# A hybrid decoder layer on one core: the branch merge passes through PSUM, and the last two experts reach their tokens by one-hot matmuls

## The chip, the core and the metric

One core of a Trainium2 chip: TensorE (PE, the matrix engine; PEld is its weight load), VectorE (DVE), ScalarE (ACT), GpSimd (POOL) and SyncE (SP, which here only issues DMAs), with SBUF and the eight banks of PSUM. The metric is the device time of one execution in microseconds. Before: 993.0 us, the median of 3 runs (991.35 to 993.85).

## The reference, cut to what matters

512 tokens of width 1024, one layer. Two things of it matter here: the merge of two attention branches, and the mixture of experts (each token goes to two of 32 experts, inside one of four groups, and their weighted outputs are added to the residual).

```python
h = rms_norm(x, g_norm_mix[l]) * (1 + scale1) + shift1
proj = h @ w_in[l]
...
g_dil, g_sb = jnp.split(jax.nn.sigmoid(h @ w_branch_gate[l]), 2, axis=-1)
merged = g_dil * (o_dil @ w_branch_dil[l]) + g_sb * (o_sb @ w_branch_sb[l])
x = x + gate1 * (merged @ w_out[l])
h2 = rms_norm(x, g_norm_ffn[l]) * (1 + scale2) + shift2
y = hierarchical_moe(h2, ...)   # silu(xe @ w_g[e]) * (xe @ w_u[e]) @ w_d[e], top-1 group, top-2 experts
x = x + gate2 * y
```

## The kernel before, in words

Each engine has its own instruction stream, written out by hand, and they meet only in semaphores. SP's queue issues nearly all loads in program order. The stages follow one another:

**Start and projections.** x is normalised and transposed; `w_ada` is multiplied by the conditioning vector in three rounds of eight pieces. Round one comes first; rounds two and three are woven into the 24 projection units (`for u in range(NU)` on TensorE): after each of the first 16 units comes one w_ada piece of 1 MB, through the single buffer `ada_slot`, whose next load SP issues when the piece has been used. Halves of `w_in` (1 MB, rows of 1 KB) are loaded between them. Weights and activations are split into a high and a low part, so each product is three fp32r passes (`split_product`, whose matmuls carry line L669). ACT makes the high part, DVE or GpSimd the low one (`split_lo`, L557 on GpSimd). `mod_round(1)` on DVE closes the second round, and copies the first gate into `grow`, which until then held the arguments of the rotary sines.

**Attention and merge.** TensorE computes the dilated and the stick-breaking attention and the gates. The merge goes over f, eight chunks of 128 channels by 512 tokens, each two products with `w_branch_sb` (`sb_product`, L853, PSUM bank f % 4). DVE multiplies by the gate (L1693), writes SBUF, and adds the other branch (L1696) into `hT`. ACT copies that to the high part (L1307), GpSimd subtracts for the low part (L581). ACT and GpSimd have the split of the second half of w_out (`split_hi(11, ..)`, `split_lo(11, ..)`) queued ahead of that. Then TensorE broadcasts the first gate over the partitions (L891), waits until ACT has copied it out (L1311), broadcasts the second (L898), computes the router bias (L906) and starts the eight output products, u = 0 to 7 (L669). DVE multiplies each by the gate (L1720) and adds x (L1724).

**Routing.** From the logits DVE makes rank tables: each expert has 64 slots (`CAP`); if an expert had more than 64 tokens, further rounds would run in `more_rounds`. Here none runs.

**Experts.** 32 experts, three weight buffers of 6 MB in `arena`. SP loads expert e + 3 as soon as TensorE has used the parts of expert e (waits on `gu_ps` and `dn_ps`); the first ones wait for `br_ps`, `o_ps` and `lg_ps`. Per expert TensorE gathers the 64 tokens' rows by a one-hot matrix (L1001), transposes them, and multiplies by gate and up (L1024); ACT and DVE compute the SwiGLU; TensorE transposes and multiplies by down (L1043). Both products use only 64 columns of the array, in pairs that run side by side. DVE weighs the result (L1886) into `ye`, GpSimd copies the expert's slot indices (L600) and stores the rows to `y_rows` in HBM by an indirect DMA (L603). `y_rows` has two rows of 512 for each of a token's two experts.

**End.** The order is in the straight-line code behind the loops: expert 31 has three idle matmuls (`keep_clock(3)`, L967) between its hT transposes (L1033) and its down product. When all 32 stores have landed, SP reloads `y_rows` in four tiles (L473), DVE adds the two y of each token to x (L1965, L1966), and SP stores the output. The sum x itself is rebuilt from its two parts by `whole_x1` (L1857).

Of the kernel before, what the change touches and what calls it, by code (L numbers as in the profile page):

```python
# [14 lines left out]
P = 128  # L15
D = 1024
# [44 lines left out]
def hybrid_layer(nc, x, c, positions, w_ada, b_ada, g_norm_mix, g_norm_ffn, w_in, w_branch_gate,  # L61
# [6 lines left out]
    with ctx:  # L68
# [161 lines left out]
        x1n = arena[:, EXP_W:EXP_W + NT * D].rearrange("p (t n) -> p t n", t=NT)  # L230
        wcol = sb("wcol", [P, 1])
# [31 lines left out]
        gn_T = sem("gn_T")  # L263
# [3 lines left out]
        mod_cols = sem("mod_cols")  # L267
# [20 lines left out]
        dil_ps, dil_ok, br_ps, merged = sem("dil_ps"), sem("dil_ok"), sem("br_ps"), sem("merged")  # L288
# [15 lines left out]
        round_seq = sem("round_seq")  # L304
        fin_ok, out_st = sem("fin_ok"), sem("out_st")
# [46 lines left out]
        def more_rounds(eng, body):  # L352

            eng.wait_ge(tables_ok, 1)
            top = eng.value_load(cnt_i[0:1, 0:1], min_val=0, max_val=SEQ - 1)
            with eng.If(top + 1 > CAP):
                with eng.Fori(1, ROUNDS) as rnd:
                    with eng.If(top + 1 > rnd * CAP):
                        body(rnd)
            return top  # L360

        @block.sync
        def _(sp):
# [105 lines left out]
            top = more_rounds(sp, sp_round)  # L469

            sp.wait_ge(y_out, (top // CAP) * (16 * NE) + 16 * NE)
            for t in range(NT):
                sp.dma_start(arena[:, 2048 * t:2048 * (t + 1)],  # L473
                             y_rows[4 * P * t:4 * P * (t + 1), :].rearrange("(p r) n -> p (r n)", r=4)
                             ).then_inc(x_in[t], 16)
            for t in range(NT):
                sp.wait_ge(fin_ok, t + 1)
# [5 lines left out]
        def _(pool):  # L483
# [24 lines left out]
            link(pool.affine_select(negstrict, negstrict, [[1, P]], ALU.is_gt, NEG, base=0, channel_multiplier=-1))  # L508

# [88 lines left out]
            def store(e, n):  # L598
                pool.wait_ge(y_ok, n + 1)
                pool.tensor_copy(idx[:], slotI[:, bass.ds(e, 1)]).then_inc(idx_ok, 1)  # L600
                pool.wait_ge(tables_ok, 1)
# [5 lines left out]

            store(0, 0)
            with pool.Fori(1, NE) as e:
                store(e, e)  # L610

# [9 lines left out]
        def _(pe):  # L621
# [9 lines left out]
            def mod_columns():  # L631
# [4 lines left out]
                mm.then_inc(mod_cols, 1)  # L636
# [16 lines left out]
            pe.transpose(ps[:, 5, 0:KC], gn_rows, ident[0:KC, 0:KC]).then_inc(gn_T, 1)  # L653
# [226 lines left out]
            for f in range(KC):  # L880
                if f >= 4:
                    pe.wait_ge(merged, f - 3)
# [12 lines left out]
            pe.wait_ge(g1_ok, 2)  # L895
            for j in range(2):
                r = 64 + 32 * j
                mm = pe.matmul(ps[64 * j:64 * j + 64, 6, :], ones[r:r + 1, 0:64], grow[r:r + 1, :],  # L898
                               start=True, stop=True)
            mm.then_inc(g_ps, 1)  # L900

            pe.wait_ge(wr_in, 16 * 4)
            pe.wait_ge(cols_in, 32)
            pe.wait_ge(cols_ok, 2)
            for k in range(KC):
                mm = pe.matmul(ps[0:1, 7, 0:NG + NE], cols[:, 3, k:k + 1], wr[:, k, :], start=(k == 0), stop=(k == KC - 1))  # L906
            mm.then_inc(b2w_ps, 1)
# [25 lines left out]
            for u in range(2 * NT):  # L933
# [15 lines left out]
                if u == 0:  # L949
                    pe.wait_ge(b2w_ok, 1)  # L950
# [150 lines left out]
            more_rounds(pe, pe_round)  # L1101
# [3 lines left out]
        def _(act):  # L1105
# [79 lines left out]
            for r in (1,):  # L1185
                act.wait_ge(mod_cols, r)
                load_bias(r)
# [115 lines left out]
            split_hi(11, 0)  # L1303
            split_hi(11, 1)
# [3 lines left out]

# [682 lines left out]
```

## Time and profile before

| | before |
|---|---|
| median of 3 runs | 993.0 us |
| profiled execution | 993.44 us |
| its span | 991.6 us |
| TensorE busy | 891.9 us (90%) |
| VectorE busy | 481.5 us (49%) |
| ScalarE busy | 195.8 us (20%) |
| GpSimd busy | 141.7 us (14%) |
| mean granted TensorE clock | 0.962 |
| HBM traffic | 263.71 MB read, 11.03 MB written |

The profile comes from one execution, taken by the hardware profiler; lines are those of the kernel before. Busy shares are means over stages with different limits, so the windows and the timeline say more. Matmuls are pipelined and overlap, so their single durations don't add up to time; the timeline gives one line for a run of instructions with its start and its whole length. A float32 matmul has two records for each matmul of the code. "idle before" is the time for which the engine stood before the instruction, with what ended it. DMA share is the mean busy share of 16 DMA engines. In the chain of waits each piece is the work that the next one waited for.

### The profile page before, as it was taken

The numbers are of one execution on the slowest core, as the hardware profiler recorded it, in microseconds if no ns is written. First come the engines' busy times: TensorE is split into PE (matmuls) and PEld (weight loads), VectorE is DVE, ScalarE is ACT, GpSimd is POOL, SyncE is SP. The second block draws the span as 40 slices with busy tenths as digits, with TensorE's granted clock in tenths as the row PEclk, the third lists the DMA queues.
The fourth block names the chain that finished last, engine by engine and source line by source line (L and its number), as shares of the span: only waits on it lengthen the run. The fifth ranks groups of instructions, "written<-read, shape, count | busy, mean of one in ns | idle before, by whom it ended". The sixth has DMA issues, their size and how long they took to land.

```text
span 991.6 us, 11091 instructions
## 1 busy us (share of the span) xinstructions
PE 891.9 (90%) x4135; PEld 513.0 (52%) x4135; DVE 481.5 (49%) x765; ACT 195.8 (20%) x328; POOL 141.7 (14%) x168
## 2 busy tenths in 40 slices
PE   3699999988989999799889999999999998989770
PEld 2376689977777665288544443444434433333220
DVE  2532556357788556723654443344433443342435
ACT  3532333334334432302200000000000000000000
POOL 1000222104223011901101000000000000000111
PEclk9799999999989999799899999999999999999985
DMA  9886763202032204324859999999999999999947
GB/s 346 303 277 211 255 223 117 86 1 92 27 99 88 85 1 169 130 125 170 337 196 422 421 421 421 421 422 421 421 421 421 422 423 422 421 422 422 423 172 262
DMA packets 59195, 271.12 MB, mean 273 GB/s; under 512 B 8824, under 2 KB 21120, under 8 KB 30996
## 3 DMA queue, kind: packets, MB, share of 16 engines
q1 hardware_dynamic: 54772, 264.41, 67.1%
q0 software_dynamic: 3072, 5.30, 1.5%
q10 hardware_dynamic: 1312, 0.87, 0.4%
q8 instruction: 28, 0.46, 0.2%
q14 instruction: 11, 0.09, 0.0%
HBM read 263.71 MB, written 11.03 MB: 277 GB/s over the span
## 4 chain that ended last, share of the span: by engine, by line
PE 39%; SPq 15%; DMA 8%; issue 2%; DVE 2%; ACT 0%; POOL 0%; POOLq 0%; DVEq 0%
SPq L422 13%; PE ps L1024 12%; PE ps L669 7%; PE ps L1043 7%; DMA arena<-in_w_expert_down 6%; PE ps L1001 4%; SPq L430 2%; PE ps L820 1%; DMA arena<-y_rows 1%; PE ps L1010 1%; PE ps L845 1%; PE ps L967 1%; PE ps L1033 1%; PE ps L829 1%; DVE arena L1693 1%
## 5 line engine op out<-in xcount | busy, mean ns | idle before, releaser
L1024 PE MATMUL ps<-arena,hT 128*64 128x512 f32 x1024 | 229.1, 596 | 6.1 <-DMA arena<-in_w_expert_up 6.1
L1024 PEld LDWEIGHTS ps<-arena,hT 128*64 128x64 f32 x1024 | 69.7, 137 | 148.4 <-issue 132.3
L1043 PE MATMUL ps<-arena,hT 128*64 128x512 f32 x512 | 119.8, 611 | 15.2 <-DMA arena<-in_w_expert_down 15.2
L1864 DVE TENSOR_SCALAR hT<-hT 128x256 f32<-128x256 f32 x32 | 9.4, 294 | 234.9 <-ACT hT L1350 234.9
L669 PE MATMUL ps<-slot_r,xs_r 128*128 128x512 f32 x320 | 106.2, 404 | 0.4 <-issue 0.4
L669 PE MATMUL ps<-xs_r,slot_r 128*128 128x512 f32 x320 | 103.8, 406 | 2.7 <-DVE hT_r L1448 2.7
L669 PE MATMUL ps<-slot_r,hT_r 128*128 128x512 f32 x224 | 88.7, 396 | 0.0
L669 PEld LDWEIGHTS ps<-slot_r,xs_r 128*128 128x128 f32 x320 | 77.1, 261 | 10.5 <-ACT arena L1210 2.5
L1043 PEld LDWEIGHTS ps<-arena,hT 128*64 128x64 f32 x512 | 34.6, 139 | 80.1 <-issue 60.9
L669 PEld LDWEIGHTS ps<-xs_r,slot_r 128*128 128x128 f32 x320 | 60.3, 194 | 19.0 <-issue 5.0
L600 POOL COPY idx<-small 128x1 int32 (+1 forms) x32 | 7.8, 243 | 421.8 <-DVE hT L1886 421.8
L669 PE MATMUL ps<-hT_r,slot_r 128*128 128x512 f32 x160 | 63.7, 398 | 0.0
L1346 ACT ACTIVATE hT<-ps,slot_rstd 128x512 f32<-128x512 f32 x32 | 22.0, 687 | 204.2 <-PE ps L1001 204.2
L557 POOL TENSOR_TENSOR slot_r<-arena,slot_r 128x2048 fp32r<-128x2048 f32 x10 | 46.7, 4675 | 94.2 <-ACT slot_r L1163 94.1
L669 PEld LDWEIGHTS ps<-slot_r,hT_r 128*128 128x128 f32 x224 | 54.5, 243 | 4.7
L1421 DVE TENSOR_TENSOR slot_r<-arena,slot_r 128x2048 fp32r<-128x2048 f32 x14 | 32.0, 2289 | 51.1 <-ACT slot_r L1163 51.1
L1866 DVE RECIPROCAL hT<-hT 128x256 f32<-128x256 f32 x32 | 56.1, 1753 | 1.1
L1350 ACT ACTIVATE hT<-ps 128x256 f32<-128x256 f32 x32 | 12.3, 385 | 223.2 <-PE ps L1024 223.2
L1613 DVE RECIPROCAL arena<-arena 128x512 f32<-128x512 f32 x16 | 53.6, 3353 | 0.5
L1001 PE MATMUL ps<-xs_r,hT_r 128*128 128x512 f32 x128 | 53.7, 419 | 0.0
L1001 PE MATMUL ps<-xn_r,hT_r 128*128 128x512 f32 x128 | 51.1, 399 | 0.0
L1163 ACT ACTIVATE slot_r<-arena 128x2048 fp32r<-128x2048 f32 x24 | 45.5, 1904 | 4.8 <-DMA arena<-in_w_in 3.1
(271 smaller groups left out, 1073.3 us busy)
## 6 DMA issues: line engine op xcount, KB each, us to landing
arena<-in_w_expert_gate SPq DMA_DIRECT2D x64, 1024.0 KB, 24.9
arena<-in_w_expert_up SPq DMA_DIRECT2D x64, 1024.0 KB, 26.9
arena<-in_w_expert_down SPq DMA_DIRECT2D x32, 2048.0 KB, 29.4
xn<-in_w_ada SPq DMA_DIRECT2D x16, 1024.0 KB, 4.9
arena<-in_w_in SPq DMA_DIRECT2D x12, 1024.0 KB, 7.8
arena<-in_w_ada SPq DMA_DIRECT2D x8, 1024.0 KB, 14.0
arena<-in_w_branch_gate SPq DMA_DIRECT2D x4, 2048.0 KB, 8.1
xs<-in_x SPq DMA_DIRECT2D x8, 512.0 KB, 8.5
```

The source lines that it names most:

```text
L422: sp.dma_start(w_gu(b)[:, g, ks].rearrange("p k n -> p (k n)"), src).then_inc(gu_in[b][kh], 16)
L430: sp.dma_start(w_dn(b).rearrange("p (h k) n -> p h (k n)", h=2), src).then_inc(dn_in[b], 16)
L557: pool.tensor_tensor(w_half(w_lo(j), j, half), w_half(w_raw(j), j, half), w_half(w_hi(j), j, half).bitcast(F32), ALU.subtract).then_inc(wl ...
L669: mm = pe.matmul(out_ps, lhsT, rhs, start=(k == 0 and i == 0), stop=(k == KC - 1 and i == 2))
L1001: mm = pe.matmul(ps[:, 6 * half, :], hot_r[:, t, :], part[:, t, half * CH:(half + 1) * CH], start=(t == 0 and part is xs_r), stop=(t == NT ...
L1024: mm = pe.matmul(ps[64 * h:64 * h + 64, 2, :], xeT[:, xb, k, CAP * j:CAP * (j + 1)], w_gu(b)[:, :, k, 256 * h:256 * h + 256], start=(k == ...
L1043: mm = pe.matmul(ps[64 * h:64 * h + 64, 4, :], hhT[:, f % 2, 64 * (f // 2):64 * (f // 2) + 64], w_dn(b)[:, f, h * CH:(h + 1) * CH], start= ...
L1163: act.activation(w_half(w_hi(j), j, half), w_half(w_raw(j), j, half), ACT.Copy).then_inc(whi_ok, 1)
L1346: act.activation(xe, ps[:, 6 * half, :], ACT.Copy, scale=slot_rstd[:, 0:1]).then_inc(xe_ok, 1)
L1421: dve.tensor_tensor(w_half(w_lo(j), j, half), w_half(w_raw(j), j, half), w_half(w_hi(j), j, half).bitcast(F32), ALU.subtract).then_inc(wlo ...
L1613: dve.reciprocal(gT[:, f, :], gT[:, f, :]).then_inc(gate_ok, 1)
L1866: dve.reciprocal(hh, hh).then_inc(h_seq, 1)
```

## The change

The edits, in the order of the program:

- `y_rows` is set to zero: GpSimd clears `grow` once the sines are done and stores it 16 times over by a DMA of 2048 rows of 2 KB. DVE waits for this DMA before it copies the first gate into `grow`.
- Merge: the multiply writes back into its PSUM bank, and the add reads the bank. TensorE's wait for a free bank is on the add (`m_full`), not the multiply.
- ACT and GpSimd split the second half of w_out behind the merge's own copies and subtractions (on ACT behind the gate copies too). The second gate's broadcast and the router bias move behind output product 0, the bias' broadcast behind product 1.
- End: experts 30 and 31 aren't stored. Their weighted rows stay in SBUF (`y_last`). TensorE transposes the one-hot matrix of the last pair ahead of expert 31, ACT copies it out (`hotT`), and at the end 16 matmuls with 64 rows of contraction bring the rows to their tokens in all eight PSUM banks; DVE adds these banks to x. The other rows are reloaded as soon as store 29 has landed (`load_y`). DVE adds them before: tile 0 ahead of the weighting of expert 31, tiles 1 to 3 behind it. If more rounds run, the reload is done again behind them. The three idle matmuls are gone. `whole_x1` runs beside experts 29 and 30.

```diff
+            pool.wait_ge(trig_ok, 2)
+            link(pool.memset(grow[:], 0.0))
+            pool.dma_start(y_rows.rearrange("(p r) n -> p r n", p=P),
+                           grow[:].unsqueeze(1).to_broadcast([P, 4 * SEQ // P, CH])).then_inc(zero_out, 16)
...
                 if r == 1:
+                    dve.wait_ge(zero_out, 16)
                     dve.tensor_copy(grow[0:64, :], modr[0:64, :]).then_inc(gates_kept, 1)
...
-            for j in (9, 10, 11):
+            for j in (9, 10):
                 for half in range(2):
                     split_lo(j, half)
             for f in range(KC):
                 pool.wait_ge(mhi_ok, f + 1)
                 pool.tensor_tensor(h_lo[:, f, :], hT[:, f, :], m_hi[:, f, :].bitcast(F32), ALU.subtract
                                    ).then_inc(mlo_ok, 1)
+            for half in range(2):
+                split_lo(11, half)
...
                 if f >= 4:
-                    pe.wait_ge(merged, f - 3)
+                    pe.wait_ge(m_full, f - 3)
...
-            pe.wait_ge(g1_ok, 2)
-            for j in range(2):
...
+            def second_gate_and_bias():
...
                 mm.then_inc(o_ps, 1)
                 if u == 0:
+                    second_gate_and_bias()
+                if u == 1:
                     pe.wait_ge(b2w_ok, 1)
...
-            split_hi(11, 0)
-            split_hi(11, 1)
             for f in range(KC):
                 act.wait_ge(m_full, f + 1)
                 act.activation(m_hi[:, f, :], hT[:, f, :], ACT.Copy).then_inc(mhi_ok, 1)
-
             act.wait_ge(g_ps, 1)
             for j in range(2):
                 act.activation(gate1b[:, j * CH:(j + 1) * CH], ps[:, 6 + j, :], ACT.Copy).then_inc(g1_ok, 1)
+            split_hi(11, 0)
+            split_hi(11, 1)
...
-                dve.tensor_tensor(gT[:, KC + f, :], gT[:, KC + f, :], ps[:, f % 4, :], ALU.mult).then_inc(merged, 1)
-                dve.wait_ge(merged, f + 1)
+                sb_ps = ps[:, f % 4, :]
+                link(dve.tensor_tensor(sb_ps, gT[:, KC + f, :], sb_ps, ALU.mult))
                 dve.wait_ge(dil_ok, KC)
-                dve.tensor_tensor(hT[:, f, :], gT[:, f, :], gT[:, KC + f, :], ALU.add).then_inc(m_full, 1)
+                dve.tensor_tensor(hT[:, f, :], gT[:, f, :], sb_ps, ALU.add).then_inc(m_full, 1)
```

The end, on SP, GpSimd, TensorE, ACT and DVE:

```diff
+            def load_y():
+                for t in range(NT):
+                    sp.dma_start(y_in[:, t].rearrange("p j n -> p (j n)"),
+                                 y_rows[4 * P * t:4 * P * (t + 1), :].rearrange("(p r) n -> p (r n)", r=4)
+                                 ).then_inc(x_in[t], 16)
+            sp.wait_ge(y_out, 16 * (NE - KEPT))
+            load_y()
+            more_rounds(sp, sp_round, sp_after)
             for t in range(NT):
-                sp.wait_ge(fin_ok, t + 1)
+                sp.wait_ge(fin_ok, 2 * t + 2)
                 sp.dma_start(out[0, t * P:(t + 1) * P, :], x1n[:, t, :]).then_inc(out_st, 16)
...
             store(0, 0)
-            with pool.Fori(1, NE) as e:
+            with pool.Fori(1, NE - KEPT) as e:
                 store(e, e)
+            for e in range(NE - KEPT, NE):
+                take_slots(e, e)
+                pool.wait_ge(idx_ok, e + 1)
...
-            for e in (NE - 2, NE - 1):
-                expert(e, *at(e), e // 2 % 2, e % 2, e // 2, at(e - 1), more=False)
-            keep_clock(3)
+            def transpose_hot():
+                pe.wait_ge(xe_ok, NE)
+                for j in range(2):
+                    for t in range(NT):
+                        for h in range(2):
+                            mm = pe.matmul(ps[64 * h:64 * h + 64, 6 * j, t * P:(t + 1) * P],
+                                           hot_r.bitcast(F32)[:, t, CAP * j:CAP * (j + 1)], ident[:],
+                                           start=True, stop=True, skip_group_check=True)
+                    mm.then_inc(last_ps, 1)
+            def scatter(rounds):
+                pe.wait_ge(hotT_ok, 2)
+                pe.wait_ge(y_ok, rounds * NE + NE)
+                for t in range(NT):
+                    for j in range(2):
+                        for h in range(2):
+                            mm = pe.matmul(ps[:, final_bank(t, h), :], hotT[64 * h:64 * h + 64, j, t, :],
+                                           y_last[64 * h:64 * h + 64, j, :], start=(j == 0), stop=(j == 1))
+                    mm.then_inc(last_ps, 1)
+            expert(NE - 2, *at(NE - 2), 1, 0, NE // 2 - 1, at(NE - 3), more=False)
+            transpose_hot()
+            expert(NE - 1, *at(NE - 1), 1, 1, NE // 2 - 1, at(NE - 2), more=False)
             down(NE - 1, *at(NE - 1))
...
-            more_rounds(pe, pe_round)
+            scatter(more_rounds(pe, pe_round) // CAP)
...
             sig(NE - 2)
+            for j in range(2):
+                act.wait_ge(last_ps, j + 1)
+                act.activation(hotT[:, j].rearrange("p t n -> p (t n)"), ps[:, 6 * j, :], ACT.Copy).then_inc(hotT_ok, 1)
             sig(NE - 1)
...
+            def add_y(t, step, loads=1):
+                dve.wait_ge(x_in[t], 32 + loads * 16)
+                for j in range(2):
+                    step(dve.tensor_tensor(x1n[:, t, :], x1n[:, t, :], y_in[:, t, j, :], ALU.add))
...
+            add_y(0, link)
+            weigh(NE - 1, NE - KEPT, y_last[:, 1, :])
...
+            for t in range(1, NT):
+                add_y(t, link)
+            more_rounds(dve, dve_round, dve_after)
             for t in range(NT):
-                dve.wait_ge(x_in[t], 48)
-                y = arena[:, 2048 * t:2048 * (t + 1)].rearrange("p (j n) -> p j n", j=2)
-                link(dve.tensor_tensor(x1n[:, t, :], x1n[:, t, :], y[:, 0, :], ALU.add))
-                dve.tensor_tensor(x1n[:, t, :], x1n[:, t, :], y[:, 1, :], ALU.add).then_inc(fin_ok, 1)
+                dve.wait_ge(last_ps, 2 + t + 1)
+                for h in range(2):
+                    part = x1n[:, t, h * CH:(h + 1) * CH]
+                    dve.tensor_tensor(part, part, ps[:, final_bank(t, h), :], ALU.add).then_inc(fin_ok, 1)
```

## Rows read from the trace of the kernel before

**Rows 1.** The page, part 4: the chain that ended last, share by engine.
```profile
PE 39%; SPq 15%; DMA 8%; issue 2%; DVE 2%; ACT 0%; POOL 0%; POOLq 0%; DVEq 0%
```

**Rows 2.** Windows, expert stage: length, busy of PE, PEld, DVE, ACT, POOL, clock, DMA, GB/s.
```profile
540.00:600.00 60.00, 60.00 (x281) 24.29 (x281) 24.01 (x43) 4.98 (x9) 6.33 (x10) 1.00 1.01 421
...
900.00:940.00 40.00, 31.95 (x146) 11.07 (x144) 15.71 (x26) 1.84 (x4) 2.68 (x6) 1.00 1.01 423
```

**Rows 3.** Timeline, merge stage: start, us, engine, line, operation, tiles, count, idle.
```profile
395.23 7.99 PE L853 MATMUL ps<-arena 128*128 128x512 f32 x18 [0.68 <-ACT arena L1285]
...
397.19 10.00 POOL L557 TENSOR_TENSOR slot_r<-arena,slot_r 128x2048 fp32r<-128x2048 f32 x2 [19.47 <-ACT slot_r L1163]
...
398.51 4.31 DVE L1696 TENSOR_TENSOR hT<-arena 128x512 f32<-128x512 f32 x1
...
402.75 0.68 DVE L1693 TENSOR_TENSOR arena<-arena,ps 128x512 f32<-128x512 f32 x1
...
407.15 12.55 POOL L581 TENSOR_TENSOR hT_r<-hT,slot_r 128x512 fp32r<-128x512 f32 x8
...
412.10 2.08 PE L891 MATMUL ps<-grow,ones 1*128 1x512 f32 x4
...
415.09 1.04 DVE L1696 TENSOR_TENSOR hT<-arena 128x512 f32<-128x512 f32 x1
...
417.96 1.97 PE L898 MATMUL ps<-grow,ones 1*64 1x512 f32 x4 [3.78 <-ACT arena L1311]
...
419.86 1.12 PE L906 MATMUL ps<-wr,cols 128*1 128x36 f32 x16
```

**Rows 4.** Chain of waits, first output products: start, us, what.
```profile
420.98 7.43 PE ps L669 x24
428.75 24.71 PE ps L669 x108
```

**Rows 5.** Chain of waits, tail.
```profile
918.77 32.48 DMA arena<-in_w_expert_down
...
951.29 6.55 PE ps L1043 x16
...
958.27 2.58 PE ps L967 x6
960.85 3.61 PE ps L1043 x16
...
964.48 0.76 DVE hT L1886
...
968.21 4.00 DMA y_rows<-hT,idx
...
973.57 12.52 DMA arena<-y_rows
...
987.37 1.23 DVE arena L1966
```

**Rows 6.** Timeline, tail.
```profile
958.75 0.41 DVE L1874 COPY hT<-ps 128x256 f32<-128x256 f32 x1
...
976.94 1.23 DVE L1965 TENSOR_TENSOR arena<-arena 128x1024 f32<-128x1024 f32 x1 [7.25 <-DMA arena<-y_rows]
```

**Rows 7.** Timeline, TensorE, dilated scores with 64 rows of contraction.
```profile
255.97 1.13 PE L746 MATMUL ps<-arena 64*128 64x256 f32 x8
```

**Rows 8.** Windows of the early projections.
```profile
60.00:72.00 12.00, 11.91 (x59) 7.91 (x59) 3.48 (x2) 3.00 (x3) 0.00 (x0) 1.00 0.66 212
72.00:84.00 12.00, 12.00 (x60) 8.08 (x59) 0.00 (x0) 2.83 (x3) 0.00 (x0) 1.00 0.96 326
```

**Rows 9.** Timeline, the second-round load that PE waited for.
```profile
61.66 0.16 PEld L627 LDWEIGHTS ps<-xn,crep 128*32 128x32 f32 x8 [0.52 <-DMA xn<-in_w_ada]
```

**Rows 10.** The page, part 6: DMA issues, KB each, us to landing.
```profile
xn<-in_w_ada SPq DMA_DIRECT2D x16, 1024.0 KB, 4.9
...
y_rows<-hT,idx POOLq DMA_INDIRECT x32, 6.7
```

More of the change, by code:

```diff
@@ L350, in later, with final_bank, more_rounds @@
             return not isinstance(e, int) or e > 0
-        def more_rounds(eng, body):
+        def final_bank(t, h):
+            return ((0, 6), (1, 7), (2, 3), (5, 4))[t][h]
+        KEPT = 2
+        def more_rounds(eng, body, after=None):
             eng.wait_ge(tables_ok, 1)
@@ L359, in more_rounds @@
                         body(rnd)
+                if after is not None:
+                    after(top // CAP)
             return top
@@ L596, in _, with take_slots, store @@
             last_row = pool.to_reg(4 * SEQ - 1)
-            def store(e, n):
+            def take_slots(e, n):
                 pool.wait_ge(y_ok, n + 1)
                 pool.tensor_copy(idx[:], slotI[:, bass.ds(e, 1)]).then_inc(idx_ok, 1)
+            def store(e, n):
+                take_slots(e, n)
                 pool.wait_ge(tables_ok, 1)
@@ L893, in _ @@
             mm.then_inc(g_ps, 1)
-            pe.wait_ge(g1_ok, 2)
-            for j in range(2):
[L897 to L907, printed above, removed]
+            def second_gate_and_bias():
+                pe.wait_ge(g1_ok, 2)
+                for j in range(2):
+                    r = 64 + 32 * j
+                    mm = pe.matmul(ps[64 * j:64 * j + 64, 6, :], ones[r:r + 1, 0:64], grow[r:r + 1, :],
+                                   start=True, stop=True)
+                mm.then_inc(g_ps, 1)
+                pe.wait_ge(wr_in, 16 * 4)
+                pe.wait_ge(cols_in, 32)
+                pe.wait_ge(cols_ok, 2)
+                for k in range(KC):
+                    mm = pe.matmul(ps[0:1, 7, 0:NG + NE], cols[:, 3, k:k + 1], wr[:, k, :], start=(k == 0), stop=(k == KC - 1))
+                mm.then_inc(b2w_ps, 1)
             def transpose_x1(t):
@@ L1184, in _ @@
             exp_and_ln()
-            for r in (1,):
-                act.wait_ge(mod_cols, r)
-                load_bias(r)
+            act.wait_ge(first_T, 2)
+            load_bias(1)
             def store_qk(u):
@@ L1726, in _ @@
                 if u == 0:
+                    dve.wait_ge(b2w_ps, 1)
+                    dve.tensor_tensor(br[:], br[:], ps[0:1, 7, 0:NG + NE], ALU.add).then_inc(b2w_ok, 1)
+                    dve.tensor_tensor(wr[:], wr[:], cols[:, 2, :].unsqueeze(2).to_broadcast([P, KC, NG + NE]), ALU.mult
+                                      ).then_inc(b2w_ok, 1)
+                if u == 1:
                     dve.wait_ge(b2w_ps, 2)
@@ L1914, in _ @@
                     expert(i * 4 + e, e % 2, i * 2 + e // 2, e // 2 % 2)
-            for e in range(NE - 4, NE):
+            expert(NE - 4, 0, NE // 2 - 2, 0)
+            for e in range(NE - 3, NE):
+                silu_up(e)
                 if e == NE - 3:
-                    silu_up(e)
                     store_xT(e + 2, 1, 1)
-                    weigh(e - 1)
-                    slot_weight(e, e)
-                    keep_hT(e)
-                else:
-                    expert(e, e % 2, e // 2, e // 2 % 2, more=(e < NE - 2))
-                if e == NE - 2:
-                    whole_x1(0)
-                    whole_x1(1)
-            weigh(NE - 1)
-            whole_x1(2)
-            whole_x1(3)
+                weigh(e - 1, min(e - 1, NE - KEPT), y_last[:, 0, :] if e - 1 == NE - 2 else ye)
+                slot_weight(e, e)
+                keep_hT(e)
+                if e < NE - 1:
+                    for t in range(2):
+                        whole_x1(2 * (e - (NE - 3)) + t, link)
+            add_y(0, link)
+            weigh(NE - 1, NE - KEPT, y_last[:, 1, :])
             def dve_round(rnd):
-                dve.wait_ge(y_out, rnd * (16 * NE))
+                dve.wait_ge(idx_ok, rnd * NE)
+                dve.wait_ge(y_out, rnd * (16 * NE) - 16 * KEPT)
                 at = [0]
```

51 lines of the change are left out of this document (26 added, 25 removed).

## The prediction

> **What bounds the kernel now.** I read the chain of waits first: PE holds 39% of the span on it, SP's queue 15% and the expert loads' landing about 6% more [rows 1]. Next the windows of the expert stage, for which of the two binds where: in 540 to 600 us PE is busy 60.00 of 60.00 us and the DMA share is 1.01; in 900 to 940 PE is busy only 31.95 of 40.00 and the share is still 1.01, at 423 GB/s [rows 2]. So up to about 720 us TensorE leads, and then the stream of expert weights does. But the loads of that stream are themselves started by events of the stages before (br_ps, o_ps, lg_ps, gu_ps), and once started the stream never pauses. A microsecond saved on TensorE before about 480 us therefore starts every later load a microsecond sooner and reaches the end in full, although the end is DMA bound. Last come the two stretches that the change edits, the merge and the tail, and the early stage where it adds a transfer. The profiled execution took 993.44 us for a span of 991.6, so 1.84 us lie outside; I sum against 993.44, which is 0.4 above the median of 993.0.
>
> **Merge stage.** Before, each of eight chunks is a product on PE, a DVE multiply (PSUM and SBUF in, SBUF out), a DVE add of two SBUF tiles, an ACT copy and a GpSimd subtraction. The add takes 4.31 us for two chunks running while GpSimd's split of w_out's second half is under way (10.00 us for two instructions), and 1.04 after that, beside GpSimd's subtractions (8 in 12.55 us); the multiply, with an operand in PSUM, takes 0.68 even there [rows 3]. After, both DVE operations have one operand in PSUM, so I price both at 0.69 and a chunk at 1.45 with the gaps. PE makes one 512-column f32 product per 7.99/9 = 0.89 us, and two per chunk from chunk 3 on, 1.78: PE leads now. Its last product of the loop ends at 395.23 + 13 x 0.89 = 406.8; the before row L891, right behind the loop, starts at 412.10. PE's new wait at chunk 4 and up is for the add instead of the multiply. That is 0.7 later, but chunk 0's add is done at about 397.9 and PE reaches chunk 4 at 399.7, so it costs nothing. Behind it in PE's queue stand only the next products. The last add ends near 408.3, against 416.13 before.
>
> Next, gates and first output product. Before, PE does L891 (2.08), idles 3.78 us for ACT's two copies, does L898 (1.97) and L906 (1.12), and starts the output product at 420.98, at half clock: its 24 matmuls take 7.43 us, against 24.71 x 24/108 = 5.49 at full clock; the next starts at 428.75 [rows 3, 4]. After, product 0 follows L891 directly and L898 and L906 come behind it. PE stays fed, so I take full clock: L891 1.05, ending at 407.9; product 0 5.5, ending at 413.4; L898 half of 1.97, L906 1.1 and about 0.2 of hand-over, so that product 1 starts at 415.75. That is 13.0 us earlier. Cover: the last ACT copy (0.63 in the timeline) ends at 409.1 and GpSimd's last subtraction (1.3 without DVE beside it) at 410.4, and product 0 wants it at 407.9 + 7 x 0.69 = 412.7. ACT's split of w_out's second half, now behind the gate copies, ends by 414, and GpSimd's, behind its subtractions, by about 422; product 4 wants them at 415.75 + 3 x 5.49 = 432. The bias tables now wait behind product 0 on DVE, with 5 us of slack. Bounds of this gain: if the clock falls as before, product 0 and the small products lose 3 and about 1, so 9.0; 13.5 at best. I keep 13.0.
>
> **Tail.** Before: the last down load lands and down(30) runs 951.29 to 957.84 at half clock; three matmuls that compute nothing run 2.58; down(31) 3.61, weighting 0.76, then index copy, the scattered store (4.00 to landing), four reloads (the last lands 12.52 after its issue) and the last add, 987.37 + 1.23 = 988.60; the last out store ends the span 3.0 later [rows 5]. After: the reload waits for stores 0 to 29 only. Store 29 is issued at about 940 and lands by about 947 to 949, so the reload queues behind the last weights, which end near 953. The first reloaded tile was usable 4.7 us after its issue before [rows 6], so tile 0 is there at about 956 and tile 3 at about 964. The y adds of tile 0 (2 x 1.23) sit in front of the weighting of expert 31 on DVE; they run 959.2 to 961.7, inside down(31). DVE's hT copy ends at 959.16 [rows 6], down(31) starts there, 1.6 earlier, since the three matmuls are gone, and ends at 962.9 at full clock, to which the clock had risen before 960.85 with PE busy from 951.29. The weighting ends at 963.7. The new transposes of the one-hot (16 products of 128 columns, 8 pairs x 4 passes x 0.055 = 1.8 us) run near 938.4, just before the first half of gate/up(31), whose second half waits for its load anyhow; ACT's copies are long before its next exp. Price nothing.
>
> The scatter is 16 products with 64 rows of contraction, in pairs on separate row halves. The trace has such pairs: four products of 256 columns in 1.13 us [rows 7], against 4 x 0.44 in series. So four pairs of two make 8 x 0.85 = 6.8, ending at 970.6. DVE is busier: the y adds of tiles 1 to 3 (6 x 1.24 = 7.4) to 971.1, the branch on the count about 1.0 (an estimate from the 0.75 us that GpSimd's queue spends between index copy and store), then 8 adds of 512 columns from PSUM at the multiply's 0.68 plus a gap [rows 3], 5.8, to 977.9. The last store adds 3.0: 980.9 against 991.6, a gain of 10.6. DVE sets this, so even a serial scatter (13.6) costs under 1.5. Bounds: if the clock is low from down(31) on, down is 2.9 and the scatter 6.8 later, giving a gain of about 6.5; if down(30) happens to find the full clock, 2.9 more, 13.5.
>
> **The fill.** New: y_rows must be zero, 4.19 MB written from grow by a GpSimd DMA of 2048 rows, issued at about 55 us, when the timeline has the sines done. GpSimd has nothing else to do until 98. DVE now waits for its landing at 97.7 ahead of the copy into grow, with the q/k units queued behind. At the 423 GB/s of the expert stream [rows 2] it is 9.9 us of all DMA engines. There PE uses one 1 MB w_ada load per projection unit of 6.67 us; such a load lands in 4.9 us, of the 5.3 between its issue (behind the last piece's use) and its turn, and already at 61.66 PE waited 0.52 for one [rows 9, 10]. The DMA share is 0.66 in 60 to 72 and 0.96 in 72 to 84, so only 4.1 + 0.5 = 4.6 us are free [rows 8]. Ends: 0 (all in gaps) and 9.9 (all ahead of the loads). I take 9.9 - 4.6 = 5.3, less the 0.4 of slack in each of two loads, 4.5, nearer to the middle because the loads also queue behind w_in halves of 1 KB rows.
>
> What the rows show of sharing is small stores: they land in 6.7 us under the full stream, 4.00 without it [rows 5, 10]. The Trainium skill (DMA: Bandwidth & Descriptors, Queues, rings and completion order) says that each DMA engine takes turns between queues packet by packet. This speaks against a free fill; by it neither 0 nor the full 9.9 would be paid. The two rows agree in that the stores are slowed and not blocked.
>
> **Sum.** 993.4 - 13.0 - 10.6 + 4.5 = 974.3; against the median 0.4 less, 974.
>
> **Rivals.**
> 1. The fill goes into gaps and costs at most 2: 971. For it: 84 to 96 us has much free DMA time. Against: the load that had no slack at 61.66.
> 2. The fill takes the loads' place in full, or its stalls also drop the clock: 10 instead of 4.5, 980.
> 3. The tail gives less: the clock is low through down(31) and scatter, or tile 0 lands after 961 and the adds queued ahead of expert 31's weighting hold it. 4 less, 978. That would be the rival in which the one-hot path doesn't shorten the end as it says.
> 4. Slower: the fill lands late. The indirect stores move 256 KB in 6.7 us, 39 GB/s; at that rate the fill takes 107 us and lands at 162. DVE stands at 97.7; PE runs dry near 110, when the first q/k transposes want DVE's result, and loses 162 + 6 - 110 = 58: 993.4 - 23.6 + 58 = 1028. It turns slower than before once the fill lands after about 128 us, below 58 GB/s. For it: it is the only rate of that queue in the trace. Against: 6.7 is mostly latency of a small transfer.
>
> **How the numbers follow.** Forecast 0.61, rivals 0.15, 0.11, 0.08 and 0.05. What this measurement can tell from no change is 0.3%, 3 us. All but rival 4 are faster: 0.95. Of rival 4's 0.05 I give 0.01 to about the same and 0.04 to slower. Range: low 967 (no fill cost and full clock in down(30): 993.4 - 13.0 - 10.6 - 2.9), high 984 (fill 9.9 and a low clock in the tail: 993.4 - 13.0 - 6.5 + 9.9); it leaves out rival 4 and corners.
>
> **What would show it.** DVE's add in the merge at 0.69 each and PE's products 0.89 apart; L891's successor at once, product 1 starting about 13 less the fill's cost before 428.75, and the expert loads shifted by the same; PE waiting for w_ada between 55 and 90 us, some 4.5 in sum; the fill landing before 97; in the tail the reload's issue before down(30), no DVE wait for it, and 6.8 us of scatter with DVE the later. The prediction is wrong if the merge adds stay long, if the stream's end does not move with the merge, or if DVE waits for the fill.

## The result, and the profile after

The changed kernel takes 983.0 us (median of 4 runs, 980.0 to 984.1) against 992.5 before: ratio 0.990, 95% interval 0.987 to 0.993. It is 9.5 us faster, where 19 were forecast; the time lies inside the range of 967 to 984, near its upper end. The profiled execution took 983.72 us for a span of 981.8, so I compare spans: 991.6 to 981.8, 9.8 less.

The span falls into stages with sharp edges in both traces, and one table tells where the time went. The edges are: the first w_ada piece in the projections; GpSimd's last memset of the slot tables; the first multiply of the merge; the gating of the last output product; the start of down(30), which waits for the last full load of the weight stream but one; the end. Each entry is a difference of two start times in the timelines.

| us | before | after | difference |
|---|---|---|---|
| start to the first w_ada piece | 48.16 | 48.92 | +0.8 |
| projections, with the fill (to the memset at 183.14, 194.44) | 134.98 | 145.52 | +10.5 |
| attention (to the merge's first multiply, 396.47, 412.02) | 213.33 | 217.58 | +4.3 |
| merge and output products (to 473.47, 475.84) | 77.00 | 63.82 | -13.2 |
| routing and experts (to down(30), 951.29, 953.84) | 477.82 | 478.00 | +0.2 |
| from down(30) to the end | 40.31 | 27.96 | -12.4 |
| span | 991.6 | 981.8 | -9.8 |

So both gains came in full and a little over, and the fill and the attention stage took 14.8 back.

**The fill's place.** Timeline of after, TensorE's weight loads for w_ada (start, us, engine, line, tiles, count, idle before), where [rows 9] had one wait of 0.52:

```profile
63.58 0.16 PEld L658 LDWEIGHTS ps<-xn,crep 128*32 128x32 f32 x8 [1.66 <-DMA xn<-in_w_ada]
78.37 0.20 PEld L658 LDWEIGHTS ps<-xn,crep 128*32 128x32 f32 x8 [8.44 <-DMA xn<-in_w_ada]
107.17 0.16 PEld L658 LDWEIGHTS ps<-xn,crep 128*32 128x32 f32 x8 [0.82 <-DMA xn<-in_w_ada]
```

Waits of 55 to 125 us (who waited for what: us in total, times, longest), and the page's part 6 (KB each, us to landing):

```profile
PE ps L658 <- DMA xn<-in_w_ada: 9.7, 3, 8.0
```
```profile
y_rows<-grow POOLq DMA_DIRECT2D x1, 4096.0 KB, 22.5
```

Windows of the same stretch, against [rows 8] (length; busy PE, PEld, DVE, ACT, POOL; clock, DMA share, GB/s):

```profile
60.00:72.00 12.00, 9.11 (x43) 6.19 (x41) 4.59 (x2) 3.25 (x4) 0.00 (x0) 1.00 0.98 366
72.00:84.00 12.00, 5.62 (x21) 3.30 (x22) 0.00 (x0) 0.00 (x0) 0.00 (x0) 0.72 0.72 281
```

The fill is in flight for 22.5 us from 56.9 on; from 56 to 76 us the channel is nearly full (DMA share 0.88 to 1.04), and the w_ada load issued at 64.71 lands at 78.3, 13.6 us later, where 4.9 was usual before. PE's busy time falls from 12.00 to 5.62 us in the second window. Its granted clock averages 0.72 there, the lower level (1.2 GHz) for part of it, and the eight products at 78.4 take 1.94 us instead of 1.07. DVE's wait for the fill's landing, at 109, cost nothing.

**Attention.** No line of this stage was changed. Windows of before and then of after, of PE alone:

```profile
240.00:255.00 15.00, 11.40 (x60) 0.89 0.42 150
255.00:270.00 15.00, 14.08 (x84) 1.00 0.12 37
```
```profile
240.00:255.00 15.00, 13.17 (x81) 1.00 0.06 14
255.00:270.00 15.00, 14.55 (x62) 0.66 0.42 155
```

The same work, some 11 us later, gets 0.66 instead of 0.89 to 1.00 of the clock: in 257 to 265 us the grant is 0.50 throughout. Over the whole stage the clock record has the lower level for 23.9 us, against 10.2 before. This is 4 us that my sum had no term for.

**Merge.** PE, DVE and GpSimd of after, against [rows 3]:

```profile
410.79 11.43 PE L884 MATMUL ps<-arena 128*128 128x512 f32 x26 [0.68 <-ACT arena L1341]
422.14 1.13 PE L922 MATMUL ps<-grow,ones 1*128 1x512 f32 x4
...
428.87 1.07 PE L931 MATMUL ps<-grow,ones 1*64 1x512 f32 x4
429.87 0.68 PE L939 MATMUL ps<-wr,cols 128*1 128x36 f32 x16
```
```profile
414.08 0.69 DVE L1755 TENSOR_TENSOR hT<-arena,ps 128x512 f32<-128x512 f32 x1
...
422.98 0.69 DVE L1755 TENSOR_TENSOR hT<-arena,ps 128x512 f32<-128x512 f32 x1
```
```profile
414.18 6.59 POOL L603 TENSOR_TENSOR hT_r<-hT,slot_r 128x512 fp32r<-128x512 f32 x5 [20.91 <-ACT slot_r L1361]
...
427.33 9.37 POOL L579 TENSOR_TENSOR slot_r<-arena,slot_r 128x2048 fp32r<-128x2048 f32 x2 [1.62 <-ACT slot_r L1220]
```

One unbroken run of 26 records on PE, all adds at 0.69 us, product 0 at once behind L922 and at full clock. Counted from the merge's first multiply, product 1 starts 13.7 us sooner than before; 0.5 of it is gone again by the last product.

**Tail.** The chain of waits of after, against [rows 5], and DVE's timeline from its wait for the reload on:

```profile
906.80 31.52 DMA arena<-in_w_expert_down
938.36 3.68 PE ps L1078 x16
942.06 0.76 DVE hT L1951
943.93 8.62 DMA y_rows<-hT,idx
952.58 8.65 DMA arena<-y_rows
961.25 1.24 DVE arena L1924
```
```profile
961.25 2.48 DVE L1924 TENSOR_TENSOR arena<-arena 128x1024 f32<-128x1024 f32 x2 [2.44 <-DMA arena<-y_rows]
963.77 0.75 DVE L1951 SCALAR_TENSOR_TENSOR arena<-ps,wcol,modr 128x512 f32<-128x512 f32 x1
964.44 7.51 DVE L1924 TENSOR_TENSOR arena<-arena 128x1024 f32<-128x1024 f32 x6
973.56 4.87 DVE L2038 TENSOR_TENSOR arena<-arena,ps 128x512 f32<-128x512 f32 x8 [1.61 <-issue]
```
```profile
953.84 3.65 PE L1078 MATMUL ps<-arena,hT 128*64 128x512 f32 x16 [1.90 <-DMA arena<-in_w_expert_down]
...
958.91 3.65 PE L1078 MATMUL ps<-arena,hT 128*64 128x512 f32 x16 [0.98 <-DVE hT L1939]
964.58 7.14 PE L1135 MATMUL ps<-arena 64*128 64x512 f32 x32 [2.02 <-DVE arena L1951]
```

The chain no longer runs through down(30) and down(31). It runs through store 29 and the reload, 17.3 us in series beside them, and DVE then has no gap but the branch. The scatter (7.14, ending at 971.7) is covered.

### The profile page after: what moved, and what is told of

Read it like the earlier page. It is cut to its first block, busy times and chain, and to the rows that moved or that the text cites. A ratio compares the mean times of both kernels' runs of the same rounds, so it can differ in the third digit from the quotient of the medians.

```text
span 981.8 us, 11215 instructions
## 1 busy us (share of the span) xinstructions
PE 897.0 (91%) x4193; PEld 518.4 (53%) x4193; DVE 478.6 (49%) x773; ACT 197.2 (20%) x330; POOL 138.0 (14%) x168
## 4 chain that ended last, share of the span: by engine, by line
PE 41%; SPq 15%; DMA 5%; DVE 2%; issue 1%; ACT 0%; DVEq 0%; POOL 0%; POOLq 0%
PE ps L1059 14%; SPq L433 12%; PE ps L700 7%; PE ps L1078 7%; PE ps L1036 4%; DMA arena<-in_w_expert_down 3%; SPq L441 2%; PE ps L884 1%; PE ps L851 1%; PE ps L1045 1%; PE ps L876 1%; DVE arena L1924 1%; DMA arena<-y_rows 1%; DMA y_rows<-hT,idx 1%; PE ps L1068 1%
## 5 line engine op out<-in xcount | busy, mean ns | idle before, releaser
L700 PEld LDWEIGHTS ps<-slot_r,xs_r 128*128 128x128 f32 x320 | 77.7, 263 | 11.5 <-issue 3.1
```

What stands on the lines that cost most here:

```text
L700: mm = pe.matmul(out_ps, lhsT, rhs, start=(k == 0 and i == 0), stop=(k == KC - 1 and i == 2))
```

## Experiments

The kernels ran in four groups, each beside the kernel before, which took 994.7, 991.2, 994.7 and 991.6 us in them, so times of different groups can differ by 3 us for no reason of the kernel. Ratios are to before in the same group. Below, "stage" means a row of the table above; stage lengths come from each run's timeline.

**The parts alone.** One kernel with all but the early fill (the same fill placed behind the rotary work, at 185 us, from `modr`; the reader of its semaphore moves too):

```diff
-            pool.wait_ge(trig_ok, 2)
-            link(pool.memset(grow[:], 0.0))
-            pool.dma_start(y_rows..., grow[:]...).then_inc(zero_out, 16)
...
             pool.wait_ge(slot_consts, 3)
+            pool.wait_ge(gates_kept, 2)
+            link(pool.memset(modr[:], 0.0))
+            pool.dma_start(y_rows..., modr[:]...).then_inc(zero_out, 16)
```

> The changed kernel with its zero fill moved: GpSimd clears modr (free after the third modulation round) and issues the same 2048-row fill at about 190 us, where the DMA share was near zero; DVE no longer waits for it, ACT waits for it before it writes gate2h. Theory A (the early fill was served ahead of the w_ada loads and cost about 10.5 us of the 15.6 us by which the merge started late): 983.0 - 10.5 = 972.5, no PE wait for w_ada over 1 us. Theory B (the fill cost the 4.5 of my sum, the rest comes from elsewhere in the change): 978.5.

Measured 971.5 us, ratio 0.977 (0.974 to 0.980). Theory A; the longest wait of PE for w_ada is 0.4 us.

The kernel before with the early fill and its waits added and nothing else:

```diff
+            pool.wait_ge(trig_ok, 2)
+            link(pool.memset(grow[:], 0.0))
+            pool.dma_start(y_rows..., grow[:]...).then_inc(zero_out, 16)
...
+                    dve.wait_ge(zero_out, 16)
                     dve.tensor_copy(grow[0:64, :], modr[0:64, :]).then_inc(gates_kept, 1)
```

> The kernel before with only the early fill of y_rows and DVE's wait for it. Theory A: 992.5 + 10.5 = 1003, with one PE wait of about 8 us for w_ada near 70 us. Theory B: 997. The slower rival of the prediction (DVE or PE held by the late landing of the fill): 1010 or more.

Measured 1006.9 us, ratio 1.012 (1.009 to 1.016), so 12.2 us more than before in its group, where theory A has 10.5. PE waits 9.9 us for w_ada, 7.9 of them at once: theory A.

The kernel before with only the merge's edits (the PSUM operands, the order of split and gates):

```diff
-                dve.tensor_tensor(gT[:, KC + f, :], gT[:, KC + f, :], ps[:, f % 4, :], ALU.mult).then_inc(merged, 1)
+                link(dve.tensor_tensor(sb_ps, gT[:, KC + f, :], sb_ps, ALU.mult))
...
+                if u == 0:
+                    second_gate_and_bias()
```

> The kernel before with only the merge edits (PSUM in place, the split of w_out's second half behind the subtractions, second gate and bias behind output product 0). Theory A: the traces' 13.8 us in full, 979, output product 1 starting about 415. Theory B, in which part of what the merge saves comes back before the end: 984.

Measured 981.6 us, ratio 0.988 (0.985 to 0.992), 13.1 us less than before in its group: theory A.

The changed kernel with the old merge and the late fill, so the tail alone:

```diff
+            split_hi(11, 0)
+            split_hi(11, 1)
             for f in range(KC):
                 act.wait_ge(m_full, f + 1)
...
+                link(dve.tensor_tensor(gT[:, KC + f, :], gT[:, KC + f, :], ps[:, f % 4, :], ALU.mult))
...
+                dve.tensor_tensor(hT[:, f, :], gT[:, f, :], gT[:, KC + f, :], ALU.add).then_inc(m_full, 1)
```

> The changed kernel with the late fill of the run before it, and with the merge, the splits' order and the gates' order as in the kernel before (only that TensorE waits for the add, not the multiply, since no semaphore is free). So it is the kernel before plus tail edits and a late fill. Theory A: 992.5 - 10 (the end of the last add relative to down(30), 12.7 in the traces, of which 2.9 are the clock level that down(30) happened to meet) = 982. Theory B: the late fill costs as well, 986.

Measured 980.9 us, ratio 0.988 (0.985 to 0.991), 13.9 us less than before in its group. The late fill shows no price, so not theory B, and the gain is larger than theory A's 10, which left the clock of down(30) out. The edits of the tail were not taken apart: what the one-hot matmuls, the earlier reload and the missing idle matmuls are worth singly is not shown.

The stages of the profiled executions, in the order of the table:

| us | before | fill only | merge only | tail only | all, fill late | after |
|---|---|---|---|---|---|---|
| projections | 134.98 | 146.16 | 134.14 | 133.90 | 134.64 | 145.52 |
| attention | 213.33 | 217.58 | 214.01 | 211.50 | 211.37 | 217.58 |
| merge, output products | 77.00 | 77.06 | 63.81 | 76.40 | 63.82 | 63.82 |
| routing, experts | 477.82 | 477.82 | 483.34 | 480.77 | 483.02 | 478.00 |
| from down(30) on | 40.31 | 40.17 | 39.91 | 27.94 | 27.98 | 27.96 |

Three rows are steps: the fill is worth 11 us in the projections, the merge's edits 13.2, the tail's 12.4, whatever else is in the kernel. The other two wander by 4 to 6 us though the edits don't touch them. That is wide enough for the times of the parts not to add up (-13.1 - 13.9 + 12.2 = -14.8, against -9.5), and what wanders comes next.

**The wandering stages.** The clearest pair is a kernel that was made for another question: the late-fill kernel with one edit in its last 20 us.

```diff
-            add_y(0, link)
             weigh(NE - 1, NE - KEPT, y_last[:, 1, :])
+            add_y(0, link)
```

> The late-fill kernel with the adds of tile 0 of the reload behind the weighting of expert 31 instead of ahead of it. Theory A, the weighting waits behind DVE's 2.4 us wait for the reload, and it stands in the chain at the end: it now runs before the reload lands, and 0.8 us (its own 0.75) to 2 us go: 970. Theory B, DVE waits for the reload anyway and PE's scatter has slack: the same time within 0.5 us, 971.5.

Measured 971.9 us, ratio 0.978 (0.973 to 0.982), the same as the late-fill kernel, so theory B by the number. Up to the last 20 us the two programs are one. Yet this one took 217.31 us for the attention stage against 211.37, entered the routing stage 5.06 us later (464.16 against 459.10), and started down(30) at the same 942.12. Windows of 5, 5 and 15 us from the last output product on, of before, of the late-fill kernel and of this one (busy PE, clock, DMA share, GB/s):

```profile
473.47:478.47 5.00, 4.01 (x34) 1.00 0.81 272
478.47:483.47 5.00, 5.00 (x14) 0.66 1.00 359
483.47:498.47 15.00, 12.21 (x51) 0.89 0.83 350
```
```profile
459.10:464.10 5.00, 4.01 (x31) 0.91 0.78 265
464.10:469.10 5.00, 5.00 (x14) 0.50 0.73 251
469.10:484.10 15.00, 13.02 (x43) 0.74 0.92 388
```
```profile
464.16:469.16 5.00, 4.01 (x35) 1.00 0.80 272
469.16:474.16 5.00, 5.00 (x14) 0.66 0.99 362
474.16:489.16 15.00, 12.18 (x51) 0.89 0.83 348
```

Of the 14 profiled kernels five show the first pattern of clock (before, after, fill only, this one and the paced fill below), and in all five routing and experts take 477.8 to 478.0 us. Five show 0.91 to 0.93 and then 0.50, and take 483.0 to 483.3; four lie between, at 480.1 to 481.6. The expert loads go out when PE has used the weights before them, so PE's delay passes on to the stream: in the first 450 us from the last output product 180.7 MB are moved with the second pattern, 182.9 with the first. So 5 us of a stage without an edit hang on the granted clock. The clock records of all 14 traces agree. In routing and experts the lower level lasts 6.8 us in the five of the first pattern, 20.5 in the five of the second, and 13.7 to 17.1 in the four between. In the attention stage 3.4 us of it go with 211.4 to 211.5 us of stage, 10.2 with 212.8 to 214.0, 17.1 to 20.5 with 214.7 to 216.1, and 23.9 with 217.3 to 217.6. Why the chip grants it so in one execution and not in the next no run here shows.

The question that the kernel was made for: from down(30) to the end it takes 29.3 us against 28.0. With the weighting in front, DVE stands idle until down(31) ends at 950.9 although the reload must have landed (in the late-fill kernel, with down(30) at the same time, it did at 949.5); with tile 0's adds in front it uses that time. In the traces the order of the change is the better one, by 1.3 us, which the times of the runs can't tell, and rival 3's held-up weighting has no price.

**What the merge's gain is made of.** Three single undoings in the late-fill kernel. The SBUF merge again:

```diff
-                link(dve.tensor_tensor(sb_ps, gT[:, KC + f, :], sb_ps, ALU.mult))
+                link(dve.tensor_tensor(gT[:, KC + f, :], gT[:, KC + f, :], ps[:, f % 4, :], ALU.mult))
...
-                dve.tensor_tensor(hT[:, f, :], gT[:, f, :], sb_ps, ALU.add).then_inc(m_full, 1)
+                dve.tensor_tensor(hT[:, f, :], gT[:, f, :], gT[:, KC + f, :], ALU.add).then_inc(m_full, 1)
```

> The late-fill kernel (971.5 us) with the merge's gate product written back to SBUF again, so that the add reads two SBUF operands; the new order (split of chunk 11 behind, second gate behind product 0) is kept. Theory A, the PSUM operand is the gain: the adds take 4.3 us each beside GpSimd as before, and some 11 of the merge stage's 13.8 us come back: 982. Theory B, the order is the gain (GpSimd's long subtraction no longer runs beside the merge): the adds take about 1.05 us, four of them hidden under PE, and the time is 973.

Measured 972.0 us, ratio 0.981 (0.978 to 0.984); merge stage 63.82 us, to the hundredth that of the late-fill kernel. Theory B. The split ahead again:

```diff
-            for j in (9, 10):
+            for j in (9, 10, 11):
...
-            for half in range(2):
-                split_lo(11, half)
```

> The late-fill kernel (971.5 us) with the split of chunk 11 ahead again as before the change; the PSUM merge is kept. Theory A: an add that reads PSUM does not wait for GpSimd, so the 12.6 us subtraction beside it costs nothing: 971.5 within 1.5. Theory B, it is the subtraction that held the adds: 977 or more, with adds above 2 us.

Measured 973.1 us, ratio 0.982 (0.979 to 0.984); merge stage 67.70 us, 3.9 more. The adds stay at 0.69, as theory A says, but it missed the price: GpSimd's subtractions of the merge queue behind the split, and PE waits for them. The chain of waits of this kernel:

```profile
399.39 9.06 POOL slot_r L579 x2
408.46 9.94 POOL hT_r L603 x8
...
418.53 0.93 PE ps L698 x3
```

Both undone at once (both diffs above):

> The late-fill kernel with both the SBUF merge and the split of chunk 11 ahead, as before the change; only the gates stay behind product 0. Theory A, each of the two edits alone takes away the same wait (DVE's add beside GpSimd's long subtraction), so only undoing both brings it back: the adds take 4.3 us beside it, the end of product 0 comes 8.6 us later than in the late-fill kernel (13.8 less the 5.2 of the gates), time 979 to 981. Theory B, the single effects add (0 for the one, 3.9 us for the other): 975.

Measured 977.9 us, ratio 0.984 (0.978 to 0.990); merge stage 71.31 us, 7.5 more. The time lies between the theories, and its interval holds both; the adds are long again and 7.5 is well above 3.9, so it is theory A, with a size somewhat smaller than its 8.6. DVE of this kernel and, for the same add, of the one with the SBUF merge alone:

```profile
400.46 4.29 DVE L1752 TENSOR_TENSOR hT<-arena 128x512 f32<-128x512 f32 x1
...
405.39 4.28 DVE L1752 TENSOR_TENSOR hT<-arena 128x512 f32<-128x512 f32 x1
```
```profile
399.55 1.05 DVE L1754 TENSOR_TENSOR hT<-arena 128x512 f32<-128x512 f32 x1
```

The second gate and the bias in front of product 0 again:

```diff
+            second_gate_and_bias()
...
                 if u == 0:
-                    second_gate_and_bias()
```

> The late-fill kernel (971.5 us) with the second gate and bias ahead of product 0 again; merge and split as in the change. Theory A: DVE's two small operations and PE's bias product (1.1 us) go on the path in front of product 0, 1.1 to 2.5 us: 973.5. Theory B: PE's wait there is a stall after which the granted clock falls, 4 us or more: 976.

Measured 977.9 us, ratio 0.985 (0.981 to 0.989); merge stage 69.02 us, 5.2 more:

```profile
411.67 1.84 PE L931 MATMUL ps<-grow,ones 1*64 1x512 f32 x4 [2.22 <-ACT arena L1364]
413.45 1.12 PE L939 MATMUL ps<-wr,cols 128*1 128x36 f32 x16
414.50 0.79 PE L700 MATMUL ps<-slot_r 128*128 128x512 f32 x1
```

PE stands 2.22 us and runs at the lower clock level into product 0 (clock 0.58 in 411 to 416 us): theory B.

So 63.82 + 7.5 + 5.2 = 76.5 of before's 77.0. The order of the gates is 5.2 of the gain, the order of the split 3.9 with PSUM operands and all 7.5 without them, and the PSUM operands are worth 3.6 where the split stays ahead and nothing where it is moved. The Trainium skill (SBUF — State Buffer, SBUF: two separate sides) says that a DVE operation with two SBUF inputs and a GpSimd operation that reads SBUF need the same pair of ports, and that the one that starts second waits until the other's whole instruction is done. The traces agree: the add begun at 400.46 ends at 404.75, when the first of two splits of about 5 us each, begun at 399.14, is over; with one operand in PSUM an add takes 0.69. The PSUM operands, which the title names, could be left out.

**What the fill costs.** Three kernels with other early fills, each with its projections row and PE's wait for w_ada. Half of the fill early, half late:

```diff
-            pool.dma_start(y_rows.rearrange("(p r) n -> p r n", p=P), ...
+            pool.dma_start(y_rows.rearrange("(p r) n -> p r n", p=P)[:, 0:8], ...
```

> The late-fill kernel (971.5 us) with the first half of the zero fill (2.1 of 4.2 MB) where the change has the whole and the other half late. Theory A, the load of w_ada gives up channel time in proportion to the fill's bytes in flight: half of the 11.5 us, 977, with one w_ada piece waiting about 4 us. Theory B, the cost is one of place (any such fill in front delays the load by the same, or the load only suffers while both are in the queues): 983 as the whole, or 972 when the half is over before the load that matters.

Measured 980.4 us, ratio 0.990 (0.987 to 0.993). Projections 142.6 us, 8 more than without; PE waits 6.3 us for w_ada, 4.9 of them at once. Neither theory: half the bytes cost 8 of 11 us, more than their share and less than the whole. The whole, in eight pieces:

```diff
+            for i in range(8):
+                if i:
+                    pool.wait_ge(ada_used, KC + i)
+                pool.dma_start(y_rows...[:, 2 * i:2 * i + 2], ...).then_inc(zero_out, 16)
```

> The changed kernel (983.0 us) with its early fill cut into eight pieces of 0.5 MB, each let go at the step at which a piece of w_ada is used (about 6.7 us apart), beside the same loads and in the same stage. Theory A, the load of w_ada suffers from 4.2 MB queued at once: paced, each piece costs at most its own 1.3 us and most fit into the gaps of that stage: 971.5 to 974. Theory B, the channel of this stage has no room for 4.2 MB more: some 10 us as with the whole, 981 or more.

Measured 980.8 us, ratio 0.987 (0.983 to 0.991). Projections 146.4 us. Theory B by the number: spreading the fill saved nothing. (Three of the pieces left together at 56 us, as their counts had been reached; the other five went out 7 to 12 us apart.) But every piece starts beside a load of w_ada, so one more kernel lets each go at a landing:

```diff
-                    pool.wait_ge(ada_used, KC + i)
+                pool.wait_ge(ada2_in, 16 * (i + 3))
```

> The early fill in seven pieces again, but each let go when a piece of w_ada has landed, not when one is used (which is when the next load goes out): the bytes and the stage are the same as in the paced fill (980.8 us, where PE waited 9.2 us in sum for w_ada), only no piece starts beside a w_ada load. Theory A, the fill costs by what it lies beside: in the time between landing and the next load it costs little, PE waits under 3 us in sum and the time is 972 to 975. Theory B, the fill's bytes displace the loads' bytes wherever they are in this stage: PE waits 8 us or more, 980 or more.

Measured 981.8 us, ratio 0.989 (0.986 to 0.992). Waits and timelines of the paced and then of this kernel:

```profile
PE ps L661 <- DMA xn<-in_w_ada: 9.2, 5, 4.6
```
```profile
PE ps L660 <- DMA xn<-in_w_ada: 4.8, 8, 1.2
```
```profile
110.39 0.42 DVE L1476 COPY grow<-modr 64x512 f32<-64x512 f32 x1 [9.46 <-DMA y_rows<-grow]
```
```profile
117.49 1.12 PE L695 MATMUL ps<-ident,xn 128*128 128x128 f32 x4 [2.51 <-DVE xn L1582]
```

Neither theory as written. Counted from the first piece, the use of the tenth comes 4.3 us later than in the kernel before, against 11.0 with the paced fill: the bytes cost less than half when they don't start beside the load. But my last piece left at 106.3, DVE stood 9.46 us for its landing, PE 2.51 for DVE, and the clock was 0.80 to 0.86 in 110 to 130 us, so the projections row is 144.4, 10 more than without. The time is theory B's, but about half of the loss comes behind the tenth piece, where DVE waited for that landing, so this kernel doesn't settle what a well placed early fill would cost. The late place shows no price in any row: 971.5.

## Why the prediction was half right

- **What bounds the kernel**: right. 13.2 us gained in the merge reached down(30) in full: routing and experts take 478.0 us against 477.8. In other traces the clock took up to 5 us of it back.
- **Merge, -13.0**: measured -13.2. Adds at 0.69, PE's 26 records in 11.43 us, product 0 at once and at full clock. The reason given for the adds was only one of two sufficient ones, as the SBUF merge shows.
- **Tail, -10.6 (6.5 to 13.5)**: measured -12.4. It came about otherwise than I summed. Counted from the start of down(30), tile 0 of the reload was usable after 7.4 us where I had 4.7: the store of 29 was issued 9.9 us ahead of down(30) where I had 11.3, its 8.62 us lay within my 7 to 9, and the reload's first tile took 8.65 more. "No DVE wait for it" failed: 2.44 us. This was hidden because down(30) ran at full clock (3.65 instead of 6.55), which I had as the upper bound only. So DVE's adds began after 7.4 us, 0.5 sooner than in my sum, and from there to the end it took 20.6 us instead of 21.7: the bank adds 4.87 instead of 5.8, no gap in front of the weighting, against that the branch 1.61 instead of 1.0. All eleven kernels with the new tail have 3.65 for down(30), all three with the old one 6.4 to 6.6, so it comes with the change, for a reason that I had not foreseen. As the chain runs through the reload, the full clock is worth less than its 2.9: at half clock down(31) would end at 965.5 and hold the weighting 1.7 us (an estimate from the rows of the tail).
- **Fill, +4.5 (0 to 9.9)**: the step that failed. PE waited 9.7 us for w_ada, of which it had waited 0.8 before too, and the stalls' low clock added 1.7 (8.3 us from the use at 78.4 to the next instead of 6.67): +10.5 here, 11 in the fill-only kernel. That is rival 2, which I gave 0.11. I had subtracted the free channel time of the stretch (4.1 us + 0.5) as if the fill could choose it. The stretch has one buffer for w_ada: its next load goes out when a piece is used and must land within 5.3 us. The fill was in flight for 22.5 us and took its bytes out of exactly that interval; the gaps came later, when nothing was waiting to be loaded. The Trainium skill (DMA: Bandwidth & Descriptors, Queues, rings and completion order) has the engines take turns between queues. The trace agrees in so far as both transfers moved at once, but that is no protection: 1 MB landed 13.6 us after its issue, 77 GB/s of the 412 to 429 that the channel carried in 64 to 76 us. My sentence that by this rule the full price would not be paid was wrong.
- **Attention, +4.3**: no step of mine. It is granted clock. The stage takes 217.3 us also in the kernel with the reordered tail and no early fill, and 211.5 in the half-fill kernel, so it need not come with a fill; but both kernels with the unbroken early fill have 217.58 in their one trace, and whether the fill's shift brings that about is not shown.
- **Rival 4** (the fill lands late) is dead: 22.5 us, 186 GB/s. **Rival 3**'s wait was there, its price not. **Rival 1** fell.

In sum: the fill cost 6.0 more than forecast, attention 4.3 and the two remaining rows 1.0 that no term covered, and merge and tail gained 2.0 more. That the time lies inside the range is in part luck: the upper end was made of a full-price fill and a weak tail, and what came was a full-price fill, a strong tail and the clock in attention.

## What to carry to other kernels

Average free channel time is no budget for a transfer that can't wait. Ask which load has the least slack between its issue and its use, and whether the new transfer is in flight then; if it is, price it by its whole bytes at least (the whole fill, 9.9 us of bytes, cost 11; its half, 5.0 us, cost 8), and look for a stage without such a load (here 185 us, between rotary work and attention: 11.5 us better by the times, 13 by the ratios, for moving a few lines). And when two edits remove the same wait, undo each alone and both together before crediting one. Where a stage without edits moves by the same few microseconds as the gain in question, compare stage by stage and not by the end.

## What the runs showed of the hardware

- A DVE add of two SBUF tiles (128x512) takes 4.3 us beside GpSimd's split (128x2048, 5 us each), 1.05 beside its small subtractions (128x512), 0.69 alone; with one operand in PSUM it takes 0.69 in all three cases.
- The indirect store of expert 29's 64 slots, issued under the full weight stream, landed after 8.62 us (median of all stores 6.7), the first reloaded tile 8.65 us after its issue, against 4.7 in the kernel before, where the stream was over.
- The same instructions are granted full clock in one trace and half in another: the lower level lasts 3.4 to 23.9 us of the attention stage, which takes 211.4 to 217.6 us with it, and 6.8 to 20.5 us of routing and experts (477.8 to 483.3), one sometimes undoing the other.
